# Summing the opening mean squares over the partitions from a high and a low part of VectorE's sum

## The reference

```
def rmsnorm(x, g):
    xf = x.astype(jnp.float32)
    y = xf * lax.rsqrt(jnp.mean(xf * xf, axis=-1, keepdims=True) + EPS)
    return (y * g.astype(jnp.float32)).astype(x.dtype)

def decoder_layer(x, ...):
    x = x + 0.5 * rmsnorm(swiglu(rmsnorm(x, g[0]), ffn1 weights), g[1])
    mix, new_state = token_mixer(rmsnorm(x, g[2]), state, ...)
    x = x + rmsnorm(mix, g[3])
    x = x + 0.5 * rmsnorm(swiglu(rmsnorm(x, g[4]), ffn2 weights), g[5])
```

## Time and profile before

| what | value |
|---|---|
| median of 3 runs | 2227.61 us |
| profiled execution, its own time | 2223.14 us |
| span of the profile | 2220.1 us |
| PE busy | 2187.1 us, 99% |
| DVE, ACT, POOL busy | 893.0, 793.4, 949.0 us |
| mean granted TensorE clock | 0.993 |
| L1885, the chunk sums on DVE | 36 of them from 0.724 to 1.748 us |
| L806, the sums over partitions on PE | 24 matmuls of 0.39 us |

### The profile page before, as it was taken

One profiled execution on the slowest core, in us unless ns is written; L12 is line 12 of the kernel. 1 busy time (PEld: TensorE's weight loads), 2 busy tenths in 40 slices (PEclk: granted clock), 3 DMA queues, 4 the chain that ended last, 5 costly groups with the idle time before them and its releaser, 6 DMA issues.

```text
span 2220.1 us, 45126 instructions
## 1 busy us (share of the span) xinstructions
PE 2187.1 (99%) x19601; PEld 2138.2 (96%) x19601; DVE 893.0 (40%) x1366; ACT 793.4 (36%) x1482; POOL 949.0 (43%) x798
## 2 busy tenths in 40 slices
PE   8999999999999999999999999999999999999998
PEld 7999999999899999999999999999998899999998
DVE  6333301666356732321163332026654665333113
ACT  5333322534244633332253333235143535333322
POOL 3744444534224444444444444444332345444442
PEclk9999999999999999999999999999999999999999
DMA  4333323332233333323233233233223133332232
GB/s 122 94 93 87 102 86 90 83 73 63 59 88 101 86 95 87 88 82 93 80 94 90 86 90 99 86 91 77 70 57 99 52 115 91 87 90 86 83 92 71
DMA packets 386181, 191.94 MB, mean 86 GB/s; under 512 B 31344, under 2 KB 384896, under 8 KB 385984
## 3 DMA queue, kind: packets, MB, share of 16 engines
q1 hardware_dynamic: 385984, 189.06, 30.7%
HBM read 180.26 MB, written 8.75 MB: 85 GB/s over the span
## 4 chain that ended last, share of the span: by engine, by line
PE 93%; DVE 5%; ACT 1%; issue 0%; SPq 0%; DMA 0%; POOL 0%; ACTq 0%
PE ps L792 85%; PE ps L1023 1%; DVE xn_lo L1825 1%; DVE x L1839 1%; DVE numer L2268 1%; DVE y_ffn L1835 1%; PE ps L1273 0%; DVE ps L1861 0%; ACT xn_hi L1355 0%; DVE x L1866 0%; PE ps L1128 0%; PE ps L1170 0%; PE ps L1158 0%; DVE c_st L2241 0%; PE ps L1080 0%
## 5 line engine op out<-in xcount | busy, mean ns | idle before, releaser
L709 POOL TENSOR_TENSOR w_lo<-w_raw,w_hi 128x512 fp32r<-128x512 f32 (+1 forms) x680 | 884.9, 1306 | 1233.8 <-ACT w_hi L1344 1232.4
L792 PE MATMUL ps<-xn_hi,w_hi 128*128 128x272 f32 x3904 | 858.0, 293 | 12.7 <-DVE xn_lo L1825 7.7
L792 PE MATMUL ps<-xn_hi,w_lo 128*128 128x272 f32 x3904 | 842.5, 289 | 0.0
L792 PE MATMUL ps<-xn_lo,w_hi 128*128 128x272 f32 x3904 | 839.8, 289 | 0.0
L1344 ACT ACTIVATE w_hi<-w_raw 128x512 fp32r<-128x512 f32 (+1 forms) x680 | 416.1, 614 | 1055.6 <-PE ps L792 994.5
L792 PEld LDWEIGHTS ps<-xn_hi,w_hi 128*128 128x128 f32 x3904 | 628.1, 189 | 35.8 <-issue 18.6
L792 PEld LDWEIGHTS ps<-xn_lo,w_hi 128*128 128x128 f32 x3904 | 628.8, 189 | 0.3
L792 PEld LDWEIGHTS ps<-xn_hi,w_lo 128*128 128x128 f32 x3904 | 625.7, 190 | 0.0
L792 PE MATMUL ps<-h_hi,w_hi 128*128 128x272 f32 x1344 | 291.8, 288 | 0.0
L792 PE MATMUL ps<-h_lo,w_hi 128*128 128x272 f32 x1344 | 291.0, 287 | 0.0
L792 PE MATMUL ps<-h_hi,w_lo 128*128 128x272 f32 x1344 | 291.0, 287 | 0.0
(11 more groups left out here) (326 smaller groups left out, 1306.9 us busy)
## 6 DMA issues: line engine op xcount, KB each, us to landing
w_raw<-in_ffn_w_gate SPq DMA_DIRECT2D x168, 256.0 KB, 2.8
w_raw<-in_ffn_w_up SPq DMA_DIRECT2D x168, 256.0 KB, 2.8
w_raw<-in_ffn_w_down SPq DMA_DIRECT2D x160, 256.0 KB, 2.8
w_raw<-in_w_in SPq DMA_DIRECT2D x120, 256.0 KB, 2.9
w_raw<-in_w_out SPq DMA_DIRECT2D x32, 256.0 KB, 2.9
s_c<-in_state_mlstm_C SPq DMA_DIRECT2D x8, 512.0 KB, 5.9
out_c_s<-s_c SPq DMA_DIRECT2D x8, 512.0 KB, 5.9
tok_in<-in_x_prompt SPq DMA_DIRECT2D x4, 512.0 KB, 4.3
```

The costliest lines, as they stand in the source:

```text
L709: pool.tensor_tensor(w_lo[:, n % RING, 0:m], w_raw[:, n % RAW, 0:m], w_hi[:, n % RING, 0:m].bitcast(F32), ALU.subtract).then_inc(w_split, 1)
L792: mm = pe.matmul(pair(p)[:, a, :], w[:, q, ws], z[:, k, half(a)], start=(k == 0 and w is w_hi and z is hi), stop=(k == chunks - 1 and w is ...
```

## The change

VectorE's sum `acc` is split into `acc_hi`, an fp32r copy made by ACT, and `acc_lo`, the rest, subtracted by DVE. The matrix of ones becomes an fp32r tile that POOL copies once at the start. For each half PE adds the products of `acc_hi` and `acc_lo` in one PSUM bank, instead of one fp32 product. `acc_hi` and `acc_lo` lie over the first two chunks of `x_sq`, which have been read by then. The other sums over partitions (`pe_post_sum`, L800) keep their fp32 form.

```
+        acc_hi = at("acc_hi", [P, T], F32R, tile_at(CV))
+        acc_lo = at("acc_lo", [P, T], F32R, tile_at(CV + 1))
...
-        ones = new("ones", [P, P])
+        ones_r = new("ones_r", [P, P], F32R)
+        ones = ones_r[:].bitcast(F32)
...
-        MASKS_DONE = 4 + 60
+        MASKS_DONE = 5 + 60
...
             make(pool.memset(ones[:], 1.0))
+            make(pool.tensor_copy(ones_r[:], ones[:]))
...
         def pe_pre_sum(pe, v):
 
-            pe.wait_ge(x_summed, (DC - 1) * (v + 1))
+            pe.wait_ge(acc_low, v + 1)
             for a in range(2):
-                mm = pe.matmul(pair(3)[:, a, :], ones[:], acc[:, half(a)], start=True, stop=True)
+                pe.matmul(pair(3)[:, a, :], ones_r[:], acc_hi[:, half(a)], start=True, stop=False)
+                mm = pe.matmul(pair(3)[:, a, :], ones_r[:], acc_lo[:, half(a)], start=False, stop=True)
             mm.then_inc(xsq_done, 1)
...
-            pe.wait_ge(const_ready, 4)
+            pe.wait_ge(const_ready, 5)
...
         def act_pre(act, v):
 
+            act.wait_ge(x_summed, (DC - 1) * (v + 1))
+            act.activation(acc_hi[:], acc[:], ACT.Copy).then_inc(acc_high, 1)
             act.wait_ge(xsq_done, v + 1)
...
                 dve.tensor_tensor(acc[:], x_sq[:, 0, :] if c == 1 else acc[:], x_sq[:, c, :], ALU.add).then_inc(x_summed, 1)
+            dve.wait_ge(acc_high, v + 1)
+            dve.tensor_tensor(acc_lo[:], acc[:], acc_hi[:].bitcast(F32), ALU.subtract).then_inc(acc_low, 1)
```

More of the change, by code:

```diff
@@ L352, in program @@
         xsq_done = sem("xsq_done")
+        acc_high = sem("acc_high")
+        acc_low = sem("acc_low")
         rstd_ready = sem("rstd_ready")
```

## The result

| what | before | after |
|---|---|---|
| median | 2227.62 us (4 runs) | 2254.83 us (4 runs, 2253.75 to 2257.80) |
| ratio | | 1.0131, 95% interval 1.0117 to 1.0145 |
| span of the profile | 2220.1 us | 2252.6 us |
| mean granted clock | 0.993 | 0.989 |

The kernel became 27.2 us slower. The page of the profile after: span, busy time, and the chain's shares by engine, which answer to the earlier trace rows.

A forecast was written before the change was run, and what follows sets the result against it. The prediction took TensorE, busy 2187.1 of 2220.1 us, as the bound. Waits of 22.8 us, minus 2.5 for the shorter reduction, plus 10.0 for the clock, added 30.3 to 2227.6: forecast 2258 us, range 2247 to 2267.

The forecast's parts named there:

- Place in line: In all six openings ScalarE makes acc_hi only behind its last weight copy, which starts 0.15 to 2.35 us after TensorE's arrival.
- The size of the waits: TensorE waits ahead of the six reductions, 2.78 to 4.50 us each, 22.8 us in all.
- POOL's hold: In the four FFN openings POOL's split holds DVE's subtraction, 0.61 us each; in the two mixer openings a memset doesn't.
- The reduction: Four fp32r matmuls on TensorE take 0.50 us in place of 0.92, giving back 2.5 us over six openings.
- The clock: TensorE's clock falls to 0.50 around the six waits, costing 10.0 us in all, bounds 0 and 16.8.
- What follows: After the reduction rstd comes 2.8 us later, but TensorE reaches its product 4.0 us later, so this costs nothing.
- second wait: Rival: TensorE also waits at its third unit for the late rstd, 2 us in each of six, 2270 us; chance 0.05.
- The eleven small DVE instructions: In the first opening they stand behind the waiting subtraction on DVE; cost put at 0, bound 0.9 us.
- Slow fp32r products: Rival: the products of acc_hi and acc_lo run at the fp32 rate, 1.84 us per reduction, 2266 us; chance 0.04.
- no wait at all: Rival: acc_hi is ready before TensorE arrives in all six openings, leaving only the shorter reduction, 2225 us; chance 0.10.
- The clock held: Rival: the waits come but TensorE's clock mostly stays at 1.00, 2248 us; chance 0.15.

The follow-up runs named there:

- the copy moved alone: The changed kernel with ScalarE's copy to acc_hi moved ahead of the weight copies of blocks 12 and 13: 2227.64 us, ratio 1.0011.
- the bare wait: The kernel before, with TensorE's reduction made to wait until POOL has split block 13, no new copy, subtraction or product: 2257.64 us, ratio 1.0150.

## Why the prediction was right

Forecast 2258 us, measured 2254.8; forecast +30.3 us, measured +27.2.

*Place in line.* That ScalarE's last weight copy, later than TensorE's arrival in all six openings, sets the wait was right, and is shown by the copy moved alone (19 us of waiting gone) and by the bare wait (the cost without the work).

*The size of the waits.* Forecast 2.78, 3.06, 4.50, 3.70, 4.37 and 4.44 us, 22.8 in all; the starts came 2.83, 3.67, 4.50, 3.61, 4.16 and 4.53 us late, 23.3. The largest miss is the first mixer opening, where the load landed later than before's: the last weight copy started 1.7 us behind TensorE's arrival, not 1.04.

*POOL's hold.* Forecast 1.33 us of subtraction in the FFN openings and 0.72 in the mixer's, read from one addition beside a split and one product beside a memset; measured 1.34 and 0.72. The rule of the Trainium skill (page "SBUF — State Buffer", section "Who interferes with whom"), by which a GpSimd instruction that only writes SBUF doesn't block it, holds in both kinds.

*The reduction.* Forecast 2.5 us back, measured 1.9: the first matmul behind a wait takes 0.23 us to the next start, not 0.125.

*The clock.* This term was mis-sized: 10.0 us forecast, 6.0 in the trace. The price of one fall was near (1.4 to 1.8 against 1.5), but I let all six places fall and four did, in the one execution that was profiled; the mean granted clocks of the four executions, 0.989, 0.989, 0.988 and 0.986, suggest that the number is not the same in each. Over the kernels run, waits of 1.2 to 2.6 us at this place mostly didn't bring a fall (one of 2.08 us did), those of 2.66 to 3.51 us did or did not from place to place, and none of 3.58 us or more was without one. The bounds 0 to 16.8 us covered it.

*What follows.* No second wait came: the view of TensorE's waits after has none at the third unit. The eleven small DVE instructions of the first opening, beside no split now, took 2.1 us in place of 6.4:

```profile
49.45 0.16 DVE L1942 COPY lbw<-lb_e 128x2 f32<-128x2 f32 x1
...
51.43 0.17 DVE L1953 TENSOR_SCALAR omlb<-omlb 128x2 f32<-128x2 f32 x1
```

*The rivals.* Slow fp32r products and no wait at all are excluded by the rows above. The clock held at two places of six.

## What to carry to other kernels

A semaphore wait costs what stands ahead of the awaited instruction in its engine's own order, and not only what that instruction takes. Of the 23.3 us by which the six starts were late, about 12 passed until ScalarE was through with its last weight copy and about 11 in the copy and the subtraction; with the copy two places earlier in line, nearly all of both was hidden. So compare the start of the last instruction in line with the arrival of the engine that will wait, place by place, before adding a hand-over. If a hand-over is needed, put it ahead of instructions that wait for loads, and move the consumer by less than the slack of what depends on it. On a TensorE-bound kernel add to each long wait one stretch at the low clock: here it came with every wait of 3.6 to 5.3 us and with some shorter ones, and cost 1.5 us where it was priced.

## What the runs showed that I had not expected

**Instruction transfers delay weight loads.** A 16 KB transfer of the instruction queue (q8) falls into each opening. Of the one or two 256 KB weight loads in whose flight it starts, one as a rule lands late, after 3.5 to 4.8 us in place of 2.8, and the load behind it after up to 3.8. Not every such load does: over the eleven traces 31% of them took 3.5 us or more, and 1.6% of the loads with no such transfer. In the kernel before it happened in all six openings, so ScalarE's last weight copy, on which each wait hangs, was itself late: with the transfer elsewhere it started up to 1.7 us earlier against TensorE. Kernels with other numbers of TensorE instructions had the transfer elsewhere, so an edit can move a wait by its length alone, here by 0.8 to 1.7 us.

**Extra products made a bound engine faster.** 108 products in the waits, 13.5 us of work, took 12.7 us off. Some 6 us of that are the clock, which they kept at 1.00; 4.8 us lie with weight copies that came earlier, in three openings with the instruction transfer outside the loads; 2 us are open. What the products are worth by themselves is not shown.
